# Two-layer decoder trunk on one core: mixer units in another order, query and key products with the weights stationary, rotary on VectorE, and a reordered prologue

## The chip, the cores and the metric

The kernel runs on one core of a Trainium2 chip. The metric is the device time in microseconds: 1187.27 us as the median of 3 runs (1187.05 to 1187.82). TensorE (PE) multiplies into PSUM (8 banks of 128 partitions by 512 fp32 numbers), VectorE (DVE), ScalarE (ACT) and GpSimd (POOL) do the rest, and SyncE (SP) issues the loads of the weights.

## The reference

Two layers, 256 tokens of width 1024, all in fp32. Each layer is

```python
h = h + 0.5 * rms_norm(swiglu(rms_norm(h, g1), w_gu, w_down), g2)          # FFN 1
u = rms_norm(h, mix_pre_g)
sb_q, sb_k, sb_v, df_q, df_k, df_v, g_sb, g_df = split(u @ w_in)           # 6 x 512, 2 x 1024
z = sb_q @ sb_k.T / 8                                                      # 8 heads of 64, strictly causal
w = exp(log_sigmoid(z) + sum of log_sigmoid(-z) over later allowed keys)   # stick-breaking
y_sb = (w @ sb_v) @ w_branch_sb
dq, dk = rope(df_q), rope(df_k)                                            # 4 heads of 2 x 64
a = softmax(dq[0] @ dk[0].T / 8) - lam * softmax(dq[1] @ dk[1].T / 8)      # causal
y_df = (rms_norm(a @ df_v) * (1 - lam_init)) @ w_branch_diff
h = h + rms_norm((sigmoid(g_sb) * y_sb + sigmoid(g_df) * y_df) @ w_out, mix_post_g)
h = h + 0.5 * rms_norm(swiglu(...), ...)                                   # FFN 2
h = h + rms_norm((p @ w_ple_proj) * sigmoid(rms_norm(h, g) @ w_ple_gate), ple_post_g)
```

## The kernel before

**Units.** All weights come in units of 1 MB (128 x 2048), three slots deep. For each unit SP loads `raw`, ACT rounds it to fp32r in `w_hi` (`high`), DVE writes the rest into `w_lo` (`low`), and PE multiplies it. A product is three matmuls: high by high, high by low, low by high. Where the weights move (`exact`, L1473 to L1475, called by `wide` and `deep`), each has 512 columns and the activations of 128 tokens are stationary. In the middle steps of an FFN (`flat_gate_up`) the weights are stationary: a long matmul (L1591) moves high and low parts of all 256 tokens (512 columns), a short one (L1601) the high part (256 columns); the result is transposed (channels by tokens) and its two halves have to be added, and scaled per token by the row `r_cols`. `begin(i, u)` waits until DVE has split unit u; `units_used` gives the slot back.

**Order.** The program of each engine is written out by hand, and each engine runs its instructions in order. The mixer's loop goes over m = 0 to 22. Units 0 to 19 are the ten column blocks of w_in, two half units (rows 0 to 511, 512 to 1023) each; block j is units 2j and 2j+1. In step m PE multiplies unit m for tokens 0 to 127, does `middle(i, m)`, then tokens 128 to 255, then `behind(i, m)`; ACT and DVE in their step m prepare unit m+2, and then do what the tables place there. Stick-breaking slot 2m is in `middle`, 2m+1 in `behind`. So the small attention operations of PE stand between half units of the w_in product.

**Mixer before.** The blocks come as sb_q, sb_k, sb_v, df_q, df_k, df_v and four halves of the gates. ACT copies q and k out of PSUM with the token's scale (`keep`, L842) into `slab`; DVE copies both v (L1314); POOL turns df_q and df_k in `rope` (L577 to L585); PE transposes each of the four with 8 transposes (`turn_four`, L1692), and ACT or DVE copies the result back (L876, L1329). For each pair of stick heads there are scores (`stick_scores`, L1709 and L1712), the sum over later keys (`stick_later`, L1723 and L1724) and values (`stick_values`, L1736), in slots 12, 15, 17 and every 6 slots after; for each differential head a mask matmul in bf16 (`masked`, L1698), scores (L1749, L1752) behind unit 12, 14, 16, 18, transposes of the mixed probabilities (L1759) behind the next unit, and values (L1767 to L1770) in the middle of the one after it. DVE takes the maximum (L1323), mixes (L1344) and scales the outputs (L1278); ACT has the exponentials (L792 to L809), L813 and L823.

**Prologue before.** p and w_ple_proj come in pieces of 128 tokens and of 128 x 512: pieces 0 and 2 and x on ACT's queue, p tile 0, piece 1, p tile 1, piece 3 and then the 12 pieces of the first three FFN units on SP's. PE keeps itself busy with 13 and 5 transposes of the identity (`warm_up`, L1884) about the transpose of p tile 0 (L1877), and does `proj(0)` token tile by token tile with the transposes of x (L1520) and of the gains (L1889 to L1896) between. `high_piece` (L657) and `low_piece` (L1062, L1065) split the pieces; `keep_e` (L670) copies the projection E out of PSUM.

Of the kernel before, what the change touches and what calls it, by code (L numbers as in the profile page):

```python
# [76 lines left out]
def trunk_kernel(nc, a, out):  # L77
    with ExitStack() as ctx:
# [82 lines left out]
        ident_b = sb("ident_b", [P, P], BF16)  # L161
# [3 lines left out]
        mask_df = sb("mask_df", [P, SEQ], BF16)  # L165
# [15 lines left out]
        slab_c = tmp[:, :, W:D]  # L181

# [42 lines left out]
        kept_dve = sem("kept_dve")  # L225
# [3 lines left out]
        sb_turned = sem("sb_turned")  # L229
# [12 lines left out]
        d_score = sem("d_score")  # L242
        d_max = sem("d_max")
# [55 lines left out]
        HT_BANK, P_BANK, FIRST_P_BANK = 6, 7, 3  # L299
# [15 lines left out]
        OUT_COLS = slice(384, W)  # L315
        both_scores = ps[:, 0:2, 0:384]
        both_outs = ps[:, 0:2, OUT_COLS]
# [30 lines left out]
        def p_bank(i):  # L348
            return bank(P_BANK if i else FIRST_P_BANK).rearrange("p (k n) -> p k n", k=2)
# [36 lines left out]
        def _(sp_):  # L386
# [3 lines left out]
            load_p(0)  # L390
# [47 lines left out]
            load_pieces(U_PROJ, (1,))  # L438
            load_p(1)
            load_pieces(U_PROJ, (3,))  # L440
            for u in range(1, PIECED):
                load_pieces(u)
            for i in range(DEPTH):
# [3 lines left out]
                for m in range(20):  # L447
                    dst = raw[:, slot(U_WIN + m), :].rearrange("p (k n) -> p k n", k=4)
                    r0, c0 = (m % 2) * 4 * P, (m // 2) * W
                    src = a["w_in"][bass.ds(i, 1), r0:r0 + 4 * P, c0:c0 + W].rearrange("o (k p) n -> p (o k) n", p=P)  # L450
                    load(i, U_WIN + m, [(dst[:, k:k + 2, :], src[:, k:k + 2, :]) for k in (0, 2)])
# [19 lines left out]
        def _(pool):  # L471
# [19 lines left out]
            pool.memset(ident_b[:, :], 0.0)  # L491
            pool.memset(minus[:, :], -1.0)
            pool.memset(cap_sb[:, :, :], BIG)
            pool.memset(mask_df[:, :], 0.0).then_inc(blank, 1)
            pool.wait_ge(blank, 2)
            pool.affine_select(out=ident_b[:, :], in_=ident_b[:, :], compare_op=ALU.not_equal, fill=1.0,
                               base=0, pattern=[[-1, P]], channel_multiplier=1)

# [6 lines left out]
            for c in (0, P):  # L505

                last = pool.affine_select(out=mask_df[:, c:c + P], in_=mask_df[:, c:c + P],
                                          compare_op=ALU.is_ge, fill=NEG, base=0, pattern=[[-1, P]],
                                          channel_multiplier=1)
            last.then_inc(const_all, 1)  # L510
# [58 lines left out]
            def rope(i, k):  # L569

                for t in range(TT):
                    pool.wait_ge(kept_act, 16 * i + 2 * (2 + k) + t + 1)
                    if k or t:
                        pool.wait_ge(roped, 4 * i + 2 * k + t)
                    x = slab[:, t, :].rearrange("p (g c) -> p g c", c=64)
                    y = rope_b[:, t, :].rearrange("p (g c) -> p g c", c=64)
                    pool.tensor_tensor(slab_c[:, t, :].rearrange("p (g c) -> p g c", c=64), x,  # L577
                                       rope_c[:, t:t + 1, :].to_broadcast([P, 8, 64]), ALU.mult)
                    pool.tensor_tensor(y[:, :, 0:32], x[:, :, 32:64],
                                       rope_s[:, t:t + 1, 0:32].to_broadcast([P, 8, 32]), ALU.mult)  # L580
                    pool.tensor_tensor(y[:, :, 32:64], x[:, :, 0:32],
                                       rope_s[:, t:t + 1, 32:64].to_broadcast([P, 8, 32]), ALU.mult
                                       ).then_inc(rope_parts, 1)
                    pool.wait_ge(rope_parts, 4 * i + 2 * k + t + 1)
                    pool.tensor_tensor(slab[:, t, :], slab_c[:, t, :], rope_b[:, t, :], ALU.add).then_inc(roped, 1)  # L585

            for i in range(DEPTH):
# [11 lines left out]
                pool.wait_ge(rope_ready, 2)  # L599
                rope(i, 0)  # L600
                rope(i, 1)
# [16 lines left out]
        def _(act):  # L618
# [41 lines left out]
            def high_p(i, t=0, toks=slice(0, SEQ)):  # L660

                act.wait_ge(p_turned, nth_p(i, t))
                act.activation(p_hi[:, :, toks], p_bank(i)[:, :, toks], ACT.Copy).then_inc(p_high, 1)
# [56 lines left out]
            def keep_r(i, f):  # L720
                act.wait_ge(r_turned, 2 * i + f + 1)
                act.activation(r_cols[:, 0, :], bank(R_BANK)[:, 0:SEQ], ACT.Copy).then_inc(r_kept, 1)
# [25 lines left out]
            def ffn(i, f, u0, g0, next_unit, loads):  # L748
# [8 lines left out]
                keep_r(i, f)  # L757
# [21 lines left out]
            def stick(i, slot_):  # L779

                if slot_ in SB_VALUE:
                    n = SB_VALUE[slot_]
                    act.wait_ge(s_value, PAIRS * i + n + 1)
                    act.activation(os_hi[:, n, :].rearrange("p (t q) -> p t q", t=TT), both_outs, ACT.Copy
# [13 lines left out]
            def diff_after(i, m):  # L798
                if m >= DF_Z0 and (m - DF_Z0) % 2 == 0 and (m - DF_Z0) // 2 < DF_HEADS:
                    hd = (m - DF_Z0) // 2  # L800
                    act.wait_ge(d_max, DF_HEADS * i + hd + 1)
                    for c in range(2):
# [12 lines left out]
            def diff_mid(i, m):  # L815

                if m >= DF_P0 and (m - DF_P0) % 2 == 0 and (m - DF_P0) // 2 < DF_HEADS:
                    hd = (m - DF_P0) // 2
                    act.wait_ge(d_value, DF_HEADS * i + hd + 1)
                    if hd:  # L820
                        act.wait_ge(d_square, DF_HEADS * i + hd)
# [1137 lines left out]
```

## Time and profile before

| | |
|---|---|
| median of 3 runs | 1187.27 us |
| the profiled execution, its own time | 1187.24 us |
| its span, first to last instruction | 1185.2 us |
| what lies around the span | 2.0 us |
| granted TensorE clock, mean | 0.999 |
| DMA | 215.36 MB, mean 182 GB/s |
| first mixer | about 205 to 345 us of the span and on to the boundary |
| second mixer | about 790 to 930 us and on |

Times are from the span's start. In the chain of waits a piece reads: start, duration, engine, tile, line and how many instructions; pieces follow each other without overlap, so there they show the rate at which PE gets on. In the timeline a matmul's own duration is longer than its share of the chain, since matmuls overlap.

### The profile page before, as it was taken

Reading aid. Unit: us, or ns where it says so; the run is one execution under the profiler, and the core shown is the slowest. Engines: PE = TensorE matmul, PEld = TensorE weight load, DVE = VectorE, ACT = ScalarE, POOL = GpSimd, SP = SyncE. Lnnn points to the kernel's source line nnn. Section 1 sums busy time; section 2 is a strip of 40 time slices with the busy share of each in tenths; the row PEclk is TensorE's granted clock in tenths of the full one; section 3 lists DMA queues with packets and bytes.
Section 4 is the critical chain, followed back from the end, with each engine's and each line's share of the span. In section 5 each row is a group of like instructions: output and inputs, shape, how many; then the busy total and the mean of one; then the engine's idle time right before and its main releaser. Section 6 shows DMA issues by size and latency. Waiting matters only on the chain.

```text
span 1185.2 us, 17137 instructions
## 1 busy us (share of the span) xinstructions
PE 1173.8 (99%) x6013; PEld 984.4 (83%) x6013; DVE 848.7 (72%) x1235; ACT 719.9 (61%) x1163; POOL 92.9 (8%) x157
## 2 busy tenths in 40 slices
PE   8999999999999999999999999999999999999997
PEld 7888888888788888888888888888877888888886
DVE  5766777588667866676787776676976776767666
ACT  6655556666665755564685655576656666555555
POOL 4000000042000100000110000010600010000002
PEclk9999999999999999999999999999999999999999
DMA  8656565553345555556546565756343456556550
GB/s 269 232 183 201 171 218 192 198 178 118 132 178 178 178 196 194 191 172 230 178 158 203 175 209 178 249 162 208 114 159 133 169 178 213 175 179 206 183 196 36
DMA packets 138654, 215.36 MB, mean 182 GB/s; under 512 B 6958, under 2 KB 97904, under 8 KB 138608
## 3 DMA queue, kind: packets, MB, share of 16 engines
q1 hardware_dynamic: 135808, 208.43, 52.9%
q10 hardware_dynamic: 2576, 6.29, 1.6%
q8 instruction: 28, 0.46, 0.2%
q14 instruction: 18, 0.15, 0.0%
q0 software_dynamic: 224, 0.04, 0.0%
HBM read 213.68 MB, written 1.05 MB: 181 GB/s over the span
## 4 chain that ended last, share of the span: by engine, by line
PE 96%; ACT 2%; DVE 1%; DMA 1%; issue 0%; POOL 0%; SPq 0%; DVEq 0%; POOLq 0%; ACTq 0%
PE ps L1591 22%; PE ps L1473 19%; PE ps L1475 19%; PE ps L1474 19%; PE ps L1601 12%; PE ps L1520 2%; PE ps L1692 1%; DMA raw<-in_w_ple_proj 1%; PE ps L1723 1%; DVE w_lo L1084 0%; ACT w_hi L646 0%; PE ps L1736 0%; PE ps L1709 0%; ACT prob L804 0%; PE ps L1752 0%
## 5 line engine op out<-in xcount | busy, mean ns | idle before, releaser
L1084 DVE SCALAR_TENSOR_TENSOR w_lo<-raw,g_layer,w_hi 128x512 fp32r<-128x512 f32 (+1 forms) x504 | 369.6, 793 | 131.4 <-ACT w_hi L646 131.4
L646 ACT ACTIVATE w_hi<-raw,g_layer 128x512 fp32r<-128x512 f32 (+1 forms) x524 | 346.9, 732 | 113.5 <-PE ps L1601 97.0
L1591 PE MATMUL ps<-x_both,w_hi 128*128 128x512 f32 x1152 | 287.7, 392 | 0.0
L1473 PE MATMUL ps<-w_hi,x_both 128*128 128x512 f32 x640 | 257.4, 402 | 0.0
L1475 PE MATMUL ps<-w_hi,x_both 128*128 128x512 f32 x640 | 250.2, 391 | 0.0
L1474 PE MATMUL ps<-w_lo,x_both 128*128 128x512 f32 x640 | 249.6, 390 | 0.0
L1591 PEld LDWEIGHTS ps<-x_both,w_hi 128*128 128x128 f32 x1152 | 209.4, 189 | 39.3 <-issue 0.3
L1081 DVE TENSOR_TENSOR w_lo<-raw,w_hi 128x1024 fp32r<-128x1024 f32 x114 | 134.7, 1221 | 55.0 <-ACT w_hi L643 55.0
L643 ACT ACTIVATE w_hi<-raw 128x1024 fp32r<-128x1024 f32 x114 | 114.7, 1052 | 91.7 <-PE ps L1475 91.6
L1601 PEld LDWEIGHTS ps<-x_both,w_lo 128*128 128x128 f32 x1152 | 152.6, 191 | 8.4
L1601 PE MATMUL ps<-x_both,w_lo 128*128 128x256 f32 x1152 | 156.0, 283 | 0.0
L1473 PEld LDWEIGHTS ps<-w_hi,x_both 128*128 128x128 f32 x640 | 120.2, 188 | 27.1 <-issue 3.3
L1475 PEld LDWEIGHTS ps<-w_hi,x_both 128*128 128x128 f32 x640 | 120.1, 188 | 26.1
L1474 PEld LDWEIGHTS ps<-w_lo,x_both 128*128 128x128 f32 x640 | 120.4, 188 | 22.8
L1473 PE MATMUL ps<-w_hi,ht_hi 128*128 128x512 f32 x320 | 124.9, 390 | 0.0
L1475 PE MATMUL ps<-w_hi,ht_lo 128*128 128x512 f32 x320 | 124.6, 389 | 0.0
L1474 PE MATMUL ps<-w_lo,ht_hi 128*128 128x512 f32 x320 | 124.5, 389 | 0.0
L728 ACT ACTIVATE glu<-glu 128x512 f32<-128x512 f32 x36 | 22.8, 633 | 78.5 <-DVE glu L1130 78.5
L1475 PEld LDWEIGHTS ps<-w_hi,ht_lo 128*128 128x128 f32 x320 | 60.1, 188 | 12.5
L1474 PEld LDWEIGHTS ps<-w_lo,ht_hi 128*128 128x128 f32 x320 | 60.1, 188 | 12.4
L1473 PEld LDWEIGHTS ps<-w_hi,ht_hi 128*128 128x128 f32 x320 | 60.1, 188 | 12.3
L536 POOL TENSOR_TENSOR ms_post<-mean_post,eps_half 128x1 f32<-128x1 f32 x8 | 2.4, 305 | 548.6 <-ACT tmp L694 548.6
(217 smaller groups left out, 1008.7 us busy)
## 6 DMA issues: line engine op xcount, KB each, us to landing
raw<-in_ffn_w_gu SPq DMA_DIRECT2D x170, 512.0 KB, 4.6
raw<-in_ffn_w_down SPq DMA_DIRECT2D x88, 512.0 KB, 4.0
raw<-in_w_in SPq DMA_DIRECT2D x80, 512.0 KB, 4.6
raw<-in_w_out SPq DMA_DIRECT2D x16, 512.0 KB, 3.7
raw<-in_w_ple_gate SPq DMA_DIRECT2D x16, 512.0 KB, 4.1
raw<-in_w_branch_sb SPq DMA_DIRECT2D x8, 512.0 KB, 3.7
raw<-in_w_branch_diff SPq DMA_DIRECT2D x8, 512.0 KB, 3.7
raw<-in_ffn_w_gu SPq DMA_DIRECT2D x12, 256.0 KB, 7.6
```

The costliest lines, as they stand in the source:

```text
L643: last = act.activation(w_hi[:, s, part], raw[:, s, part], ACT.Copy)
L646: last = act.activation(w_hi[:, s, part], raw[:, s, part], ACT.Copy, scale=g_layer[:, g:g + 1])
L728: act.activation(glu_g, glu_g, ACT.Silu).then_inc(silu_done, 2)
L1081: last = dve.tensor_tensor(w_lo[:, s, part], raw[:, s, part], whi[:, part], ALU.subtract)
L1084: last = dve.scalar_tensor_tensor(out=w_lo[:, s, part], in0=raw[:, s, part], scalar=g_layer[:, g:g + 1], in1=whi[:, part], op0=ALU.mult, o ...
L1473: pe.matmul(dst, x_h, w_h, start=first, stop=False, **group)
L1474: pe.matmul(dst, x_h, w_l, start=False, stop=False, **group)
L1475: return pe.matmul(dst, x_l, w_h, start=False, stop=last, **group)
L1520: mm = pe.transpose(x_bank(i, q, idx)[:, k * P:(k + 1) * P], src[:, (4 * n + k) * P:(4 * n + k + 1) * P], ident[:, :])
L1591: mm = pe.matmul(dst, w_hi[:, s, cols], x_both[:, :, 4 * half + k, :], start=half == 0 and k == 0, stop=stop and k == 3, skip_group_check= ...
L1601: mm = pe.matmul(bank(FLAT_BANK[j])[:, 0:SEQ], w_lo[:, s, cols], x_hi[:, 4 * half + k, :], start=False, stop=False, skip_group_check=True)
L1692: mm = pe.transpose(dst[:, k * SEQ + t * P:k * SEQ + (t + 1) * P], src[:, t, k * P:(k + 1) * P], ident[:, :])
```

## The change

The column blocks of w_in come in another order (df_q, df_k, sb_q, sb_k, df_v, sb_v, gates). sb_q and sb_k are multiplied with the weights stationary (`flat_win`); ACT copies one half of each result (`keep_flat`), DVE adds the other and multiplies by the token scales (`add_flat`), which PE transposes once for it at the end of unit 2 (`turn_r`). Their `turn_four` go. Rotary moves to DVE, straight out of PSUM, and its L1314 copies of v go to ACT. The mask matmul goes; DVE caps the diagonal scores in PSUM instead, ahead of the maximum. The tables place stick scores and differential scores together behind units 7, 10, 13, 16, stick later-sums together with the differential transposes in the middle of units 9, 12, 15, 18, and the values of stick pairs in the middle of 12, behind 13 and 16, in the middle of 19, differential values behind 9, 12, 15, 18. Stick outputs have banks of their own. In the prologue the projection is done in the order in which the pieces come, p tile 1 is issued ahead of piece 1, and E is copied earlier. The wait for the first product at the first flat gate-up (banks 6, 7) is left out. At the top of the mixer DVE spreads r_pre for `turn_r`.

```diff
-SBQ, SBK, SBV, DFQ, DFK, DFV = range(6)
+DFQ, DFK, SBQ, SBK, DFV, SBV = range(6)
+W_IN_BLOCK = (3, 4, 0, 1, 5, 2, 6, 7, 8, 9)
 PAIRS = SB_HEADS // 2
-SB_SCORE = {12 + 6 * n: n for n in range(PAIRS)}
-SB_LATER = {15 + 6 * n: n for n in range(PAIRS)}
-SB_VALUE = {17 + 6 * n: n for n in range(PAIRS)}
-DF_Z0, DF_T0, DF_P0 = 12, 13, 14
-BY_ACT = (0, 1, 3, 4, 6, 7, 8, 9)
-QK_ORDER = {SBQ: 0, SBK: 1, DFQ: 2, DFK: 3}
+SB_SCORE = {15 + 6 * n: n for n in range(PAIRS)}
+SB_LATER = {18 + 6 * n: n for n in range(PAIRS)}
+SB_VALUE = {slot_: n for n, slot_ in enumerate((24, 27, 33, 38))}
+DF_SCORE = {7 + 3 * n: n for n in range(DF_HEADS)}
+DF_TURN = {9 + 3 * n: n for n in range(DF_HEADS)}
+BY_ACT = (DFV, SBV, 6, 7, 8, 9)
 PIECED = 4
-WARM_UP = (13, 5)
+WARM_UP = (13, 3)
...
+        SB_FLAT = {SBQ: (0, 4), SBK: (0, 2)}
+        VALUE_BANK = (3, 3, 3, 5)
+        def outs(n):
+            return bank(VALUE_BANK[n])[:, 0:SEQ].rearrange("p (t q) -> p t q", t=TT)
...
-            load_pieces(U_PROJ, (1,))
-            load_p(1)
-            load_pieces(U_PROJ, (3,))
+            load_pieces(U_PROJ, (1, 3))
...
-            def rope(i, k):
...
-                    pool.tensor_tensor(slab[:, t, :], slab_c[:, t, :], rope_b[:, t, :], ALU.add).then_inc(roped, 1)
...
+            def keep_flat(i, j, x):
+                wait_product(act, win_done, 10 * i + j + 1, i, U_WIN + 2 * j + 1, x)
+                act.wait_ge(flat_added, 4 * i + 2 * (j - SBQ) + x)
+                act.activation(flat_copy, flat_pair(SB_FLAT[j][x])[1], ACT.Copy,
+                               scale=SB_D ** -0.5 if j == SBQ else 1.0).then_inc(flat_kept, 1)
...
+                    elif m in (5, 7):
+                        for x in range(2):
+                            high(i, U_WIN + m + 2, 8 + 4 * (m % 2), halves=(x,))
+                            keep_flat(i, m // 2, x)
...
             high_piece(U_PROJ, 0)
             high_p(0, 0, slice(0, P))
+            high_piece(U_PROJ, 2)
+            high_p(0, 1, slice(P, SEQ))
             high_piece(U_PROJ, 1)
-            high_p(0, 1, slice(P, SEQ))
-            high_piece(U_PROJ, 2)
             high_piece(U_PROJ, 3)
             load_x(1)
             high_inputs(0, 0, 0, (0,))
             high_inputs(0, 0, 1, (0,))
             high_piece(1, 3)
             high_piece(2, 0)
+            for t in range(TT):
+                keep_e(0, t)
+            high_piece(2, 1)
             high_inputs(0, 0, 0, (1,))
-            high_piece(2, 1)
             high_piece(2, 2)
-            keep_e(0, 0)
+            high_piece(2, 3)
+            high_piece(3, 0)
+            high_piece(3, 1)
             high_inputs(0, 0, 1, (1,))
-            high_piece(2, 3)
             square_pre(0, 0, 0)
-            keep_e(0, 1)
-            for k in range(4):
-                high_piece(3, k)
+            high_piece(3, 2)
+            high_piece(3, 3)
             first_silu(0, 0, U_FFN1)
...
+            def rope(i, k, t):
+                wait_product(dve, win_done, 10 * i + k + 1, i, U_WIN + 2 * k + 1, t)
+                r = (r_query, r_pre)[k][:, t:t + 1]
+                x = bank(WIN_BANK[k][t]).rearrange("p (g c) -> p g c", c=64)
+                y = rope_b[:, t, :].rearrange("p (g c) -> p g c", c=64)
+                dve.scalar_tensor_tensor(out=slab_c[:, t, :].rearrange("p (g c) -> p g c", c=64), in0=x, scalar=r,
+                                         in1=rope_c[:, t:t + 1, :].to_broadcast([P, 8, 64]),
+                                         op0=ALU.mult, op1=ALU.mult)
+                for lo, hi in ((0, 32), (32, 64)):
+                    last = dve.scalar_tensor_tensor(out=y[:, :, lo:hi], in0=x[:, :, 32 - lo:64 - lo], scalar=r,
+                                                    in1=rope_s[:, t:t + 1, lo:hi].to_broadcast([P, 8, 32]),
+                                                    op0=ALU.mult, op1=ALU.mult)
+                last.then_inc(rope_parts, 1)
+                dve.wait_ge(rope_parts, 4 * i + 2 * k + t + 1)
+                dve.tensor_tensor(df_slabs[k][t], slab_c[:, t, :], rope_b[:, t, :], ALU.add).then_inc(roped, 1)
+            def add_flat(i, j, x):
+                n = 4 * i + 2 * (j - SBQ) + x + 1
+                dst = (sbq_t, sbk_t)[j - SBQ][:, 2 * x:2 * x + 2, :]
+                dve.wait_ge(flat_kept, n)
+                dve.scalar_tensor_tensor(out=dst, in0=flat_pair(SB_FLAT[j][x])[0],
+                                         scalar=SB_D ** -0.5 if j == SBQ else 1.0, in1=flat_copy,
+                                         op0=ALU.mult, op1=ALU.add).then_inc(flat_added, 1)
+                dve.wait_ge(flat_added, n)
+                dve.wait_ge(r_kept, nth_r(i, 1))
+                dve.tensor_tensor(dst, dst, r_cols.to_broadcast([P, 2, SEQ]), ALU.mult).then_inc(sb_ready, 1)
...
+                    if m - 1 in DF_TURN:
+                        diff_normed(i, DF_TURN[m - 1])
+                    stick_cap(i, 2 * m)
+                    if m in (1, 3):
+                        rope(i, m // 2, 1)
...
+                        for c in range(2):
+                            last = dve.tensor_tensor(diagonal(DF_BANK[c]), diagonal(DF_BANK[c]),
+                                                     cap_df[:, :, :].to_broadcast([P, 2, P]), ALU.min)
+                        last.then_inc(d_capped, 1)
+                        dve.wait_ge(d_capped, DF_HEADS * i + hd + 1)
...
-            def masked(b, mask):
-                pe.matmul(diagonal(b), ident_b[:, :], mask[:, :].rearrange("p (a n) -> p a n", a=2), start=True,
-                          stop=False, skip_group_check=True)
...
-                pe.wait_ge(sb_turned, 2 * i + 2)
+                pe.wait_ge(sb_ready, 4 * i + 3 + n // 2)
                 if n:
-                    pe.wait_ge(os_split, PAIRS * i + n)
+                    pe.wait_ge(s_weight, PAIRS * i + n)
...
+                kept(i, (SBV, SBV, 7, 8)[n], 1)
+                if n:
+                    pe.wait_ge(os_split, PAIRS * i + n)
...
+            def flat_win(i, m, j, half, x):
+                s, b = slot(U_WIN + m), SB_FLAT[j][x]
+                if half == 0:
+                    if x:
+                        pe.wait_ge(rope_parts, 4 * i + 2 * (j - SBQ) + 2)
+                    elif j == SBK:
+                        pe.wait_ge(flat_added, 4 * i + 1)
+                def long(stop):
+                    for n in range(2):
+                        dst = bank(b + n).rearrange("p (a n) -> p a n", a=2)
+                        for k in range(4):
+                            cols = slice(k * W + (2 * x + n) * P, k * W + (2 * x + n + 1) * P)
+                            mm = pe.matmul(dst, w_hi[:, s, cols], x_both[:, :, 4 * half + k, :],
+                                           start=half == 0 and k == 0, stop=stop and k == 3, skip_group_check=True)
+                    return mm
+                def short():
...
+            def bank_free(i, j, t):
+                if j in (DFV, SBV):
+                    pe.wait_ge(flat_added, 4 * i + 2 * (j - DFV) + 2)
+                elif j > SBV:
+                    kept(i, j - 2, t)
+                    if t == 1 and j in (7, 9):
+                        pe.wait_ge(os_split, PAIRS * i + {7: 2, 9: 3}[j])
...
+            def first_proj():
+                beside = {(0, 1): lambda: (turn(0, 0, 0), turn_first_gain()), (0, 3): lambda: turn(0, 0, 2),
+                          (1, 3): turn_gains}
+                for t, k in ((0, 0), (0, 2), (1, 0), (1, 2), (0, 1), (0, 3), (1, 1), (1, 3)):
+                    if (t, k) in beside:
+                        beside[t, k]()
+                    if k == 0:
+                        pe.wait_ge(p_split, nth_p(0, t))
+                    if t == 0 and k < 3:
+                        pe.wait_ge(piece_split, (0, 2, 1).index(k) + 1)
+                    if (t, k) == (0, 3):
+                        begin(0, U_PROJ)
+                    cols, toks = piece(U_PROJ, k), slice(t * P, (t + 1) * P)
+                    mm = exact(bank(E_PAIR[t] + k // 2), p_hi[:, k % 2, toks], p_lo[:, k % 2, toks],
+                               w_hi[:, slot(U_PROJ), cols], w_lo[:, slot(U_PROJ), cols], k % 2 == 0, k % 2 == 1)
+                    if (t, k) == (0, 3):
+                        mm.then_inc(e_done, 1)
+                mm.then_inc(units_used, 1)
```

ACT's `keep` now serves df_v, sb_v and the gates; ACT copies both turned df tiles (behind units 4 and 6). DVE's prologue list follows ACT's.

## Rows read from the trace of the kernel before

**Rows 1.** The page, busy time by engine: us, share of span, instructions.

```profile
PE 1173.8 (99%) x6013; PEld 984.4 (83%) x6013; DVE 848.7 (72%) x1235; ACT 719.9 (61%) x1163; POOL 92.9 (8%) x157
```

**Rows 2.** The page, the chain that ended last, by engine.

```profile
PE 96%; ACT 2%; DVE 1%; DMA 1%; issue 0%; POOL 0%; SPq 0%; DVEq 0%; POOLq 0%; ACTq 0%
```

**Rows 3.** Waits of PE: line, releaser, us in total, times, longest.

```profile
PE ps L1767 <- ACT mixed_t L813: 0.4, 2, 0.2
```

**Rows 4.** The chain of waits in the first mixer: start, us, what.

```profile
218.82 0.87 PE ps L1692 x8
...
239.68 0.63 PE ps L1709 x4
240.31 0.22 PE ps L1712 x4
240.53 0.43 PE ps L1473
...
256.37 0.43 PE ps L1473
...
284.55 0.23 PE ps L1698 x2
284.78 0.42 PE ps L1749 x4
...
295.95 0.24 PE ps L1770 x2
...
298.00 0.61 DVE glu L1278 x2
...
315.83 0.36 PE ps L1698 x2
```

**Rows 5.** The chain of waits over one step of the FFN loop.

```profile
45.33 1.81 PE ps L1591 x8
...
56.48 0.23 PE ps L1473
...
61.92 1.81 PE ps L1591 x8
```

**Rows 6.** Busy time, mixer: columns us; PE, PEld, DVE, ACT, POOL busy; clock, DMA, GB/s.

```profile
205.00:345.00 140.00, 139.79 (x729) 112.69 (x728) 101.83 (x156) 94.18 (x181) 26.29 (x29) 1.00 0.48 162
```

**Rows 7.** Groups of DVE in the first mixer: busy us, mean ns, idle before.

```profile
L1241 DVE SCALAR_TENSOR_TENSOR soft<-ps,soft 128x768 f32<-128x768 f32 x4 | 3.8, 956 | 4.1 <-ACT soft L796 4.1
```

**Rows 8.** Timeline of DVE in the first mixer: start, us, line, operation.

```profile
222.01 2.74 DVE L1084 SCALAR_TENSOR_TENSOR w_lo<-raw,g_layer,w_hi 128x512 fp32r<-128x512 f32 x4 [2.74 <-ACT w_hi L646]
...
246.44 4.78 DVE L1084 SCALAR_TENSOR_TENSOR w_lo<-raw,g_layer,w_hi 128x512 fp32r<-128x512 f32 x4
```

**Rows 9.** Groups of POOL in the first mixer.

```profile
L577 POOL TENSOR_TENSOR tmp<-tmp,rope_c 128x512 f32<-128x512 f32 x4 | 5.6, 1403 | 43.3 <-ACT tmp L842 43.0
```

**Rows 10.** Groups of ACT in the first mixer.

```profile
L845 ACT ACTIVATE gates<-ps,r_pre 128x512 f32<-128x512 f32 x8 | 5.0, 673 | 0.0
```

**Rows 11.** The chain of waits, prologue.

```profile
27.93 1.81 PE ps L1591 x8
...
30.70 2.00 PE ps L1591 x8
```

**Rows 12.** Issue to landing, two p tiles (issued 0.8, 1.7).

```profile
DMA to landing us min/median/max: 2.9/4.2/5.5
```

**Rows 13.** Issue to landing, w_ple_proj pieces 0 and 2 (issued 0.8, 1.3).

```profile
DMA to landing us min/median/max: 3.1/4.1/5.1
```

**Rows 14.** Issue to landing, first six w_gu pieces (issued 2.7 to 6.6).

```profile
DMA to landing us min/median/max: 7.6/7.6/7.9
```

**Rows 15.** Timeline of the prologue.

```profile
4.84 0.99 PE L1884 MATMUL ps<-ident 128*128 128x128 f32 x5
...
6.32 0.39 PE L1474 MATMUL ps<-w_lo,p_hi 128*128 128x512 f32 x1
...
13.35 1.32 ACT L657 ACTIVATE w_hi<-raw,g_layer 128x512 fp32r<-128x512 f32 x2
```

More of the change, by code:

```diff
@@ L181, in trunk_kernel @@
         slab_c = tmp[:, :, W:D]
+        df_slabs = [[x[:, t, 0:W] for t in range(TT)] for x in (tmp, gates[:, 0, :, :])]
+        flat_copy = w_att[:, :, 0:SEQ]
         minus = mixed_t[:, 0:P]
@@ new lines, in diff_keep, with diff_square @@
+            def diff_keep(i, hd):
+                act.wait_ge(d_turned, DF_HEADS * i + hd + 1)
+                act.activation(mixed_t[:, :], bank(DF_BANK[0])[:, 0:384], ACT.Copy).then_inc(d_kept, 1)
+            def diff_square(i, hd):
+                act.wait_ge(d_value, DF_HEADS * i + hd + 1)
+                if hd:
+                    act.wait_ge(d_square, DF_HEADS * i + hd)
+                for t in range(TT):
+                    last = act.activation(squares[:, t * P:(t + 1) * P], bank(DF_BANK[1])[:, t * P:(t + 1) * P],
+                                          ACT.Square, scale=DF_V ** -0.5, accum_out=mean_sub[:, t:t + 1])
+                last.then_inc(d_square, 1)
@@ L1285, in mixer @@
                     elif 2 * m in SB_VALUE:
-                        low(i, U_WIN + m + 2, 8 + 4 * (m % 2), halves=(0,))
+                        gain = 8 + 4 * (m % 2) if m < 18 else None
+                        low(i, U_WIN + m + 2, gain, halves=(0,))
                         stick_out(i, 2 * m)
-                        low(i, U_WIN + m + 2, 8 + 4 * (m % 2), halves=(1,))
+                        low(i, U_WIN + m + 2, gain, halves=(1,))
+                    elif m in (5, 7):
+                        for x in range(2):
+                            low(i, U_WIN + m + 2, 8 + 4 * (m % 2), halves=(x,))
+                            add_flat(i, m // 2, x)
                     elif m < 18:
@@ L1575, in ffn, with flat_gate_up @@
             def ffn(i, f, q, u0, before_last):
-                def flat_gate_up(u, half, step, c=0):
+                def flat_gate_up(u, half, step, c=0, first=False):
                     begin(i, u, c)
@@ L1580, in flat_gate_up @@
                     for js in ((0, 1), (2, 3)):
-                        if half == 0:
+                        if half == 0 and not (first and js == (0, 1)):
                             pe.wait_ge(prod_done, 4 * NC * i + 2 * NC * f + 2 * step + js[0] // 2 - 1)
@@ L1745, in diff_scores @@
                     pe.wait_ge(d_normed, DF_HEADS * i + hd)
-                for c in range(2):
-                    masked(DF_BANK[c], mask_df)
                 for c, rows in enumerate(HEAD_ROWS):
-                    pe.matmul(bank(DF_BANK[c])[:, 0:P], dfq_t[rows, hd, 0:P], dfk_t[rows, hd, 0:P], start=False,
+                    pe.matmul(bank(DF_BANK[c])[:, 0:P], dfq_t[rows, hd, 0:P], dfk_t[rows, hd, 0:P], start=True,
                               stop=False, skip_group_check=True)
@@ new lines, in flat_win @@
+            def flat_win(i, m, j, half, x):
[14 more added lines that the diff above has]
+                def short():
+                    for n in range(2):
+                        for k in range(4):
+                            cols = slice(k * W + (2 * x + n) * P, k * W + (2 * x + n + 1) * P)
+                            mm = pe.matmul(bank(b + n)[:, 0:SEQ], w_lo[:, s, cols], x_hi[:, 4 * half + k, :],
+                                           start=False, stop=False, skip_group_check=True)
+                    return mm
+                if half == 0:
+                    long(False)
+                    return short()
+                short()
+                mm = long(True)
+                if x == 0:
+                    mm.then_inc(win_done, 1)
+                return mm
```

293 lines of the change are left out of this document (123 added, 170 removed).

## The prediction

> **What bounds the kernel now.** I read the busy times first: PE is busy for 1173.8 of 1185.2 us [rows 1]. Busy time alone would not settle it, since matmuls overlap, so next the chain that ended last: 96% of it is PE [rows 2]. Then PE's waits: in both mixers together it waits 0.4 us, at two places, for ACT's copy of the turned probabilities [rows 3]. The other waits lie in the first 11 us and the tail. So only three things can move the time: the work in PE's own queue, the prologue until PE runs without a gap, and new waits that the new order makes. DVE and ACT are busy for 102 and 94 of 140 us of a mixer [rows 6]: what they gain or lose counts only where PE comes to stand.
>
> **The mixer, PE's work per layer.** Prices are steps of the chain.
>
> 1. Turns of q and k. Eight transposes take 0.87 us [rows 4]; four such groups become two: -1.74.
> 2. Masks. Four pairs of bf16 matmuls at 0.23 or 0.36 us [rows 4]; I take 0.27, nearer to the more frequent value: -1.08 (-0.9 to -1.4).
> 3. Scores beside scores. Four stick score matmuls with 128 columns take 0.22 us, four differential ones of the same shape 0.42, right behind the mask [rows 4]: 0.20 for entering the 64-row form. The first full matmul behind the stick scores takes 0.43 us [rows 4] where one takes 0.23: 0.20 for leaving it. With the two kinds of scores in a row behind units 7, 10, 13, 16, one entry and one exit go per head: 4 x 0.40 = -1.60 (0 if the cost is per group, not per change).
> 4. Values ahead of scores, behind units 13 and 16. Behind values the full matmul also takes 0.43 [rows 4]. One of the two exits goes at each place: 2 x 0.20 = -0.40 (0 to -0.8). The Trainium skill (TensorEngine Tiling, Tiling Modes, Key Properties) says that changing the tiling mode drains the array, not only changing the tile. Values and scores differ in their form, so by that rule a change stays between them and the term is 0.40; if they counted as one form it would be 0.80.
> 5. `turn_r`: two transposes, a quarter of 0.87: +0.22.
> 6. Flat blocks. A loop step takes 61.92 - 45.33 = 16.59 us, of which the down product, 24 matmuls, takes 61.92 - 56.48 = 5.44, so 0.227 each. The flat pair of units is 16.59 - 5.44 = 11.15 us [rows 5]; as a wide pair it would be 48 x 0.227 = 10.88. Two blocks: +0.54. The columns are equal in number, but the flat form has 64 instructions for 48.
> 7. A new wait. Differential values of head 0 now stand right behind unit 9, and their third group needs tile 1 of df_v, which ACT can only begin to copy when unit 9 ends. That copy takes 0.67 us [rows 10], the matmuls ahead of it about 2 x 0.22: +0.30 (0 to 0.7, if ACT is behind by one more copy). Behind it are PE's whole queue and unit 10.
>
> Sum: -1.74 - 1.08 - 1.60 - 0.40 + 0.22 + 0.54 + 0.30 = -3.76, for two layers -7.5. PE's wait for the turned probabilities goes, since the values come half a unit after the turn: -0.4 [rows 3]. The wait left out at the first flat gate-up I cost at nothing: that first group takes 1.81 us in the prologue as in the loop [rows 5, 11], so nothing waited there.
>
> **The mixer, the other engines.** Rotary is 4 instructions per token tile (512, 256, 256, 512 columns). DVE's nearest row is 956 ns for 768 columns out of PSUM [rows 7], which makes some 0.7, 0.35, 0.35, 0.7: 2.1 us, four times, 8.4 in all. Its upper bound is POOL's own 1.40 for 512 columns [rows 9], so 5.2 per tile. `add_flat` is 2 x 0.7, four times: 5.6. The caps are 8 at 0.35 to 0.45, about 3.2. The v copies and the copies of the turned df tiles leave DVE (about 5.3). Against this, four pieces of `w_lo` take 2.74 us alone and 4.78 while POOL runs rotary [rows 8], and POOL is busy for 26.3 us of this stretch [rows 6]; the Trainium skill (SBUF — State Buffer, Who interferes with whom) calls this an exclusive lock on a shared port pair, for DVE instructions with two SBUF inputs, and by it all of the excess goes. I take it as 10 us back. DVE's net is then +2 and at the upper prices +14 of 140: there is room. Cover in detail: DVE splits two units ahead of PE, 10.9 us. In steps 1 and 3 it has 2.74 + 2 x 2.1 = 6.9 us, in 2 and 4 2.74, a mean of 4.8 against PE's 5.45. Without this cover the cost is item for item: at POOL's prices steps 1 to 4 hold 32 us against 22, and nearly all of the lead is gone.
>
> The tightest new place is the first stick score, behind unit 7. SBK's first half is done in the middle of unit 7; ACT copies (0.6), DVE adds and scales (1.4), while the low half of unit 9 (1.4, behind ACT's copy of a turned tile) may stand ahead. I count 5.2 us from the start of unit 7, PE asks at 5.6: no wait, margin 0.4. The next is DVE's scaling of head n, needed by the scores of head n+1. Before, it came 298.61 - 296.19 = 2.4 us after the values with DVE idle ahead of it [rows 4]. Now ACT starts `high` of the next unit only behind the squares (0.65) and DVE scales behind its `low`: about 0.65 + 2.6 + 0.8 + 0.6 = 4.7 us after the values, and PE asks a unit later, at 5.45. Margin 0.75, at units 10, 13, 16. The copies of q and k that leave ACT (8) and those that come (4 flat, 4 v) balance.
>
> **The prologue.** p tile 1 was issued at 1.7 and landed 5.5 later, at 7.2 [rows 12]; issued 0.46 earlier and ahead of 256 KB, it lands before 6.7. Piece 2 lands at 1.3 + 5.1 = 6.4 [rows 13]; ACT splits a piece in 0.66, DVE in 0.7 [rows 8, 15], so PE has it at 7.75. From there nothing is late: seven groups of three projection matmuls and 48 of the gate-up, 69 x 0.23 = 15.9, four turns of x at 0.44 (half of 0.87), the gains 0.3: 7.75 + 15.9 + 1.75 + 0.3 = 25.7 for the first flat group, which began at 27.93 [rows 11]. The weights allow it: the w_gu pieces land from 2.7 + 7.9 = 10.6 to 6.6 + 7.6 = 14.2 [rows 14], and with ACT at 0.66 and DVE at 0.7 per piece, the copy of the gains between, piece 3 is split at about 16.0, where PE wants it at 16.1. E's copies (2 x 1 us) now stand ahead of piece 5 on ACT, where it waited for x before. Gain 2.2. The second flat group waited 0.16 for the product of token tile 1 (2.00 against 1.84) [rows 11]; ACT's chain to that product moves forward by less than PE does, to about 28.95, and the group would start at 28.5: 0.4, so +0.25. Sum -1.95 (-0.3 if a landing holds it, -2.4).
>
> **The forecast.** -7.5 - 0.4 - 1.95 = -9.9. The profiled execution took 1187.24 us, 0.03 below the median: 1177.3 us. Its own range is 1175 to 1179.5, from the bounds of items 2, 4, 7 and the prologue.
>
> **Rivals.**
>
> A. The changes of form cost nothing when joined, since the 0.20 is a start-up of each group. Then items 3 and 4 vanish: +4.0, 1181.3. For: the 0.42 stands behind a bf16 matmul, another kind of operand. Against: the exit is seen on a full matmul, which is no group of its own.
>
> B. PE's clock comes late in the prologue. The five transposes of the warm-up take 0.99 us, 0.20 each, and eight in the mixer 0.87, 0.11 each [rows 4, 15]: the first ran at the lower level (1.2 GHz), and by 6.32 a matmul takes the 0.39 us that all take [rows 15]. So the level rose just behind the warm-up. With two transposes fewer and then a gap until p tile 1 has landed, it may stay low for the first four projection groups: 12 x 0.23 more, less the 0.5 of idle time this fills, +2.3: 1179.6. The Trainium skill (TensorE: Matmul & The Clock Gate, Part 4: PE-mode transpose) says that transposes don't count as work for the gate. By that rule the warm-up never did anything and the level would always be low at the first projections; the row at 6.32 says otherwise, with only transposes before.
>
> C. The prologue is held by landings: 1178.9 to 1179.2.
>
> D. Slower. The scaling of a differential head stands behind `low`, that behind `high`, that behind the squares, and these behind PE's values, a closed loop three times per layer. It decides from 0.75 us of lateness on. If DVE's steps in which the cap (0.8), the maximum (1.0), the stick softplus (3.3) and the mixing (1.2) meet run 3 us late, each of six places costs 2.25: +13.5, 1190.8. For: these now fall in one step. Against: a head's loop has three units for it, 16.4 us and the small operations, where it had two.
>
> E. Small waits at several of these places, 3 to 6 us in all: 1180 to 1183.5.
>
> **Chances.** Forecast 0.65, A 0.08, B and C 0.10, E 0.10, D 0.07. Less than 0.2% (2.4 us) can't be told from no change here. Faster by more: forecast, A, B, C and nearly all of E, 0.89. Within: 0.04. Slower: 0.07. Range 1174.5 to 1182.5: it takes in A, B, C and half of E.
>
> **What would show it.** The first flat group at 25.7 us. In the mixer: no 0.42 for the differential 128-column scores behind stick scores; a wait of PE for ACT's copy of v_df of about 0.3; four pieces of w_lo in 2.74 throughout; no waits of PE for L1278's successor or for the token-scaled q and k. The mixer from its start to the start of FFN 2 about 4 us shorter. The forecast is wrong if PE waits for DVE in the mixer for more than 1 us per layer, or if the first matmuls of the projection are 0.46 apart.

## The result, and the profile after

The changed kernel takes 1175.96 us (median of 5 runs, 1175.88 to 1176.14) where the kernel before takes 1187.44 us on the same chip (5 runs, 1187.05 to 1187.82): ratio 0.9903 [0.9892, 0.9914], 11.5 us less. The forecast was 1177.3 us, that is 9.9 less, with a range of 1174.5 to 1182.5. The profiled execution took 1175.95 us, its span 1174.2 us. From the page, busy times and the chain that ended last by engine, the answer to [rows 1, 2]:

```profile
PE 1164.3 (99%) x6031; PEld 983.6 (84%) x6031; DVE 849.9 (72%) x1289; ACT 720.6 (61%) x1165; POOL 52.1 (4%) x122
PE 99%; ACT 0%; DVE 0%; POOL 0%; issue 0%; DVEq 0%; POOLq 0%; ACTq 0%
```

PE has 9.5 us less to do and is on 99% of the chain instead of 96%. What it waits for (us in total, times, longest), answering to [rows 3]:

```profile
PE ps L1958 <- POOL ident L489: 1.6, 1, 1.6
PE ps L1801 <- ACT v_df L827: 0.7, 2, 0.3
PE ps L1506 <- DVE p_lo L1404: 0.4, 1, 0.4
```

In the mixers the only wait is the one that item 7 announced, 0.3 per layer; the old one on the turned probabilities is gone. The first mixer in the chain of waits (start, duration, what), answering to [rows 4]. L1867 and L1876 are the long and the short matmuls of the flat blocks, L1727 is `turn_four`, L1739 and L1742 the stick scores, L1779 and L1782 the differential ones, L1768 the stick values, L1801 the third group of differential values, L1506 the first of three wide matmuls:

```profile
221.88 1.81 PE ps L1867 x8
...
239.47 0.87 PE ps L1727 x8
...
245.93 0.63 PE ps L1739 x4
...
246.79 0.22 PE ps L1779 x4
247.01 0.43 PE ps L1782 x4
247.44 0.43 PE ps L1506
...
260.06 0.70 ACT v_df L827
260.80 0.49 PE ps L1801 x2
...
288.01 0.81 PE ps L1768 x12
288.82 0.63 PE ps L1739 x4
```

The differential 128-column scores stand at 246.79 and take 0.22 behind stick scores, where they took 0.42 behind the mask. The only long step behind the two groups is one exit, 0.43 at 247.44. To place the gain in time I took the last flat group of each FFN; in front of the second FFN lies a whole mixer. Before:

```profile
170.79 1.84 PE ps L1591 x8
...
540.15 1.84 PE ps L1591 x8
```

and after:

```profile
168.13 1.84 PE ps L1626 x8
...
533.31 1.84 PE ps L1626 x8
```

2.66 us are gained before the first mixer, 6.84 behind it: the prologue gives 2.66 and the first mixer 4.18. About the second mixer the same groups stand at 755.27 and 1124.62 before, at 748.52 and 1113.69 after: 6.75 and 10.93, again 4.18. The spans differ by 11.0, so 0.1 lies in the tail. Around the span lie 1.75 us where it was 2.0 (0.3), and the last 0.2 up to the 11.5 of the medians is spread of the runs.

### The profile page after: what moved, and what is told of

Read it like the earlier page. It is cut to its first block, busy times and chain, and to the rows that moved or that the text cites. A ratio compares the mean times of both kernels' runs of the same rounds, so it can differ in the third digit from the quotient of the medians.

```text
span 1174.2 us, 17191 instructions
## 1 busy us (share of the span) xinstructions
PE 1164.3 (99%) x6031; PEld 983.6 (84%) x6031; DVE 849.9 (72%) x1289; ACT 720.6 (61%) x1165; POOL 52.1 (4%) x122
## 4 chain that ended last, share of the span: by engine, by line
PE 99%; ACT 0%; DVE 0%; POOL 0%; issue 0%; DVEq 0%; POOLq 0%; ACTq 0%
PE ps L1626 23%; PE ps L1506 19%; PE ps L1508 18%; PE ps L1507 18%; PE ps L1636 12%; PE ps L1867 2%; PE ps L1553 2%; PE ps L1876 1%; PE ps L1753 1%; PE ps L1768 1%; PE ps L1727 0%; PE ps L1739 0%; PE ps L1782 0%; PE ps L1958 0%; PE ps L1789 0%; PE ps L1801 0%
## 5 line engine op out<-in xcount | busy, mean ns | idle before, releaser
L1077 DVE SCALAR_TENSOR_TENSOR w_lo<-raw,g_layer,w_hi 128x512 fp32r<-128x512 f32 (+1 forms) x504 | 356.4, 767 | 139.0 <-ACT w_hi L632 139.0
L1506 PE MATMUL ps<-w_hi,x_both 128*128 128x512 f32 x576 | 231.1, 401 | 0.0
L1508 PE MATMUL ps<-w_hi,x_both 128*128 128x512 f32 x576 | 225.1, 391 | 0.0
L1507 PE MATMUL ps<-w_lo,x_both 128*128 128x512 f32 x576 | 224.6, 390 | 0.0
L1506 PEld LDWEIGHTS ps<-w_hi,x_both 128*128 128x128 f32 x576 | 108.2, 188 | 24.1 <-issue 3.0
L1508 PEld LDWEIGHTS ps<-w_hi,x_both 128*128 128x128 f32 x576 | 108.1, 188 | 23.5
L1507 PEld LDWEIGHTS ps<-w_lo,x_both 128*128 128x128 f32 x576 | 108.4, 188 | 20.6
L1506 PE MATMUL ps<-w_hi,ht_hi 128*128 128x512 f32 x320 | 125.0, 390 | 0.0
L1506 PEld LDWEIGHTS ps<-w_hi,ht_hi 128*128 128x128 f32 x320 | 60.1, 188 | 12.3
L1125 DVE TENSOR_TENSOR glu<-glu,prob 128x512 f32<-128x512 f32 x36 | 24.9, 692 | 27.6 <-ACT glu L714 27.6
```

The costliest lines, as they stand in the source:

```text
L1077: last = dve.scalar_tensor_tensor(out=w_lo[:, s, part], in0=raw[:, s, part], scalar=g_layer[:, g:g + 1], in1=whi[:, part], op0=ALU.mult, o ...
L1125: dve.tensor_tensor(glu_g, glu_g, wide_r, ALU.mult).then_inc(silu_scaled, 1)
L1506: pe.matmul(dst, x_h, w_h, start=first, stop=False, **group)
L1507: pe.matmul(dst, x_h, w_l, start=False, stop=False, **group)
L1508: return pe.matmul(dst, x_l, w_h, start=False, stop=last, **group)
```

## The experiments

Six of the eight kernels change one thing in the changed kernel or bring one part of it to the kernel before; e5 is a repeat and e8 joins two repairs. e1 to e4 ran beside each other, and so did e5 to e8. The changed kernel took 1175.96 for the result and 1176.37 as e5, so 0.4 us is what one kernel differs by from itself between groups, and a difference is given against both where it is small.

**e1: the prologue alone**, in the kernel before: `WARM_UP = (13, 3)`, p tile 1 ahead of piece 1, `first_proj`, E's copies early.

```diff
-            load_p(0)
+            for t in range(TT):
+                load_p(t)
...
+            for t in range(TT):
+                keep_e(0, t)
...
-            keep_e(0, 0)
...
-            keep_e(0, 1)
```

> The kernel before with the new prologue alone (load order, projection in order of arrival, E copied early, warm-up 13 and 3); the mixer as before. Theory: the gain of the prologue is its own and is kept to the end, since PE never waits afterwards. In the changed kernel the last flat group of FFN 1 ends 2.66 us earlier, so this kernel takes 2.6 us less than before, about 1184.8. Rival: the prologue only moves a wait (weights of the first mixer or the first layer's end are not there earlier), then it is within 0.5 us of before.

1184.96 us (1184.3 to 1185.46, 10 runs), ratio 0.9977 [0.9968, 0.9986] to 1187.38: 2.4 less. The first flat group began at 25.87 where it began at 27.93 [rows 11]. What the prologue gains is kept to the end. The rest is 9.0 us: 8.4 in the two mixers (2 x 4.18), and 0.6 by which the first flat group began earlier still in the changed kernel's own profile (25.31).

**e2: the two kinds of scores apart.** Three of the four stick score groups go to the middle of a unit.

```diff
-SB_SCORE = {15 + 6 * n: n for n in range(PAIRS)}
+SB_SCORE = {15: 0, 20: 1, 26: 2, 32: 3}
```

> The changed kernel with the stick scores of pairs 1, 2 and 3 half a unit earlier, in the middle of units 10, 13, 16, and the differential scores left behind these units; pair 0 stays joined. Theory (0.20 us for each change into or out of the 64-row form): 6 heads x 0.40 = +2.4 us against the changed kernel, 1178.4. Rival (joining costs and gives nothing, the 0.20 was a start-up of each group): 0, 1176.0. If an early stick score must wait for the weights of the pair before, more than +2.4.

1178.67 us (1178.49 to 1179.12, 5 runs), ratio 0.9925 [0.9911, 0.9938]: 2.7 more than the changed kernel, 2.3 more than its repeat. The chain of waits:

```profile
264.81 0.43 PE ps L1506
...
267.78 0.42 PE ps L1779 x4
...
268.64 0.43 PE ps L1506
```

The same eight differential matmuls now cost an entry of 0.20 (0.42 for 0.22) and leave behind them a second exit of 0.20 (0.43 for 0.23): 0.40, six times 2.4. That is the price of a change of form, not of a group: rival A is out.

**e3: a bf16 matmul between them.** The mask matmuls are put back behind the stick scores; DVE's cap stays, so in the mixer only PE's side changes.

```diff
+                for c in range(2):
+                    pe.matmul(diagonal(DF_BANK[c]), ident_b[:, :], mask_df[:, :].rearrange("p (a n) -> p a n", a=2),
+                              start=True, stop=False, skip_group_check=True)
```

> The changed kernel with the two bf16 mask matmuls put back ahead of each pair of differential scores, so between stick scores and differential scores; DVE's cap stays too. Theory (the 0.20 is for a change of form): 0.27 for the masks, 0.40 for one more exit and entry, 8 heads: +5.4 us, 1181.4. Rival (start-up per group): the masks alone, 8 x 0.27 = +2.2, 1178.2.

1180.53 us (1180.26 to 1180.73, 5 runs), ratio 0.9939 [0.9925, 0.9953]: 4.6 more (4.2 against the repeat).

```profile
247.01 0.33 PE ps L1789 x2
247.34 0.42 PE ps L1792 x4
247.76 0.43 PE ps L1795 x4
248.19 0.43 PE ps L1516
```

A mask in the middle costs 0.33 of its own and 0.20 for entering the scores again (L1792: 0.42), 0.53 per head and 4.2 for eight heads. I had expected 5.4, with a whole exit of 0.20 on the small matmuls; they took 0.33 behind scores where most took 0.23 behind wide ones [rows 4], 0.10 more. The change of form therefore costs both ways again, but less into a small bf16 group than into a wide matmul. The Trainium skill (TensorEngine Tiling (Array Packing), Tiling Modes, Key Properties) says that a change of mode drains the array and a change of tile doesn't; e2 and e3 agree that the changes cost time, at 0.20 us for each side of fp32 work and 0.10 into the bf16 pair.

**e4: ACT's copy of v in two parts**, head 0's 128 columns first, so that PE's third value group waits for a quarter of the copy.

```diff
+                        if (j, t) == (DFV, 1):
+                            act.activation(dst[:, 0:DF_V], bank(WIN_BANK[0][1])[:, 0:DF_V], ACT.Copy,
+                                           scale=r_pre[:, 1:2]).then_inc(kept_head, 1)
...
-                kept(i, DFV, 1)
+                if hd == 0:
+                    pe.wait_ge(kept_head, i + 1)
+                else:
+                    kept(i, DFV, 1)
```

> The changed kernel with ACT's copy of token tile 1 of df_v in two parts, the 128 columns of head 0 first, and PE's values of head 0 waiting for that part alone. Theory: in the chain of the changed kernel the new wait costs 0.70 + 0.04 + 0.49 - 0.66 = 0.57 us per layer; the first part takes about 0.3, less than the 0.44 of PE's matmuls ahead, so both waits go: -1.1 us, 1174.8. Rival: the wait only moves to the restart of PE or to ACT, whose squares come later by the second part: 0 to -0.4.

1175.65 us (1175.53 to 1175.75, 4 runs), ratio 0.9898 [0.9883, 0.9913]: 0.3 less, 0.7 less than the repeat, where 1.1 less was expected. The chain, and PE's load of the weights for the third group from the timeline:

```profile
260.62 0.22 PE ps L1805 x2
260.85 0.01 issue
260.86 0.49 PE ps L1811 x2
```

```profile
260.86 0.30 PEld L1811 LDWEIGHTS ps<-v_df,mixed_t 128*128 128x128 f32 x2 [0.20 <-ACT v_df L827]
```

The wait has shrunk to 0.01, but the third group still takes 0.49 where the two before it take 0.22 each. From the end of the unit to the next wide matmul it was 1.25 us (260.04 to 261.29) and is 0.95. So a wait has two prices in the chain: its own length, and 0.27 for starting again. The second stayed here because the first part of the copy was done only when PE had finished the group ahead: the load of the weights still stood 0.20 us for ACT. No run has the copy done early enough to show both prices gone. The kernel before has the same start on another line, its wait for the turned probabilities: there the first group of head 1 took 0.49, that of head 2, which waited for nothing, 0.22:

```profile
311.01 0.49 PE ps L1767 x2
...
326.78 0.22 PE ps L1767 x2
```

The prediction priced both waits, the old one and the new, by their length alone.

**e5: the changed kernel again**, as the measure for e6 to e8.

> The changed kernel itself, as the yardstick of this group: 1176.0 us. The start of the first flat group differs from profile to profile with the landing of the first pieces (25.2 to 25.9 us so far), so 0.3 us of spread is expected and no more.

1176.37 us (1176.21 to 1176.43, 4 runs), ratio 0.9908 [0.9893, 0.9924] to 1187.14. Its profile lists a small wait of the prologue that the first did not list. In its chain, DVE's work for the pieces of the first FFN unit (the gains are copied from 13.09 to 13.47):

```profile
14.21 0.60 DVE x_both L1102
14.81 0.67 DVE w_lo L1058
...
15.52 0.50 PE ps L1506
```

The copies of the gains and x's second tile stand ahead of the piece that PE needs next, and PE asks at 15.3. In the changed kernel's first profile the same matmul takes 0.49 (at 15.22) without a listed wait: PE came just to a stand there too. The wait is 0 to 0.2 us from one execution to the next.

**e6: POOL busy in the mixer.** Twenty products of 128 x 256 in SBUF per layer, from unit 5 on; nobody reads them.

```diff
+                for n in range(20):
+                    if i or n:
+                        pool.wait_ge(pool_step, 20 * i + n)
+                    pool.tensor_tensor(pool_out[:, :], pool_in[:, :], pool_in[:, :], ALU.mult).then_inc(pool_step, 1)
```

> The changed kernel with 20 two-input operations of 128x256 on POOL per layer, from the end of SBQ's first half (unit 5) on, on tiles that nobody reads: POOL is as busy there as it was with rotary. Theory: VectorE's time was never the limit, so the pieces of w_lo take up to 4.8 us per four again and the kernel loses nothing but at the tightest place, the first stick score (0.5 us of margin in the changed kernel): 0 to +2 us, 1176 to 1178. Rival (clearing POOL was a part of the 11.5 us): +4 us or more.

1177.38 us (1177.27 to 1177.57, 5 runs), ratio 0.9917 [0.9904, 0.9931]: 1.0 more than e5. PE's waits, the stick scores in the chain, and DVE's timeline (start, duration, line, operation) about the flat sums:

```profile
PE ps L1748 <- DVE sbk_t L1308: 1.0, 2, 0.5
```

```profile
246.67 0.70 PE ps L1748 x4
```

```profile
238.01 4.16 DVE L1086 SCALAR_TENSOR_TENSOR w_lo<-raw,g_layer,w_hi 128x512 fp32r<-128x512 f32 x4
...
245.54 1.07 DVE L1308 TENSOR_TENSOR sbk_t<-sbk_t,prob 128x512 f32<-128x512 f32 x1
```

Four pieces take 4.16 in place of 2.74, and `add_flat`'s multiplication 1.07 in place of 0.69. The first stick score (L1748) waits 0.5 per layer. That is where I had put the tightest margin, 0.4 us, and it is what breaks first. Behind the wait the scores take 0.70 where they take 0.63 without one: 0.07 more, and not 0.27, so starting again and entering the scores (0.20) are not paid one on top of the other. The Trainium skill (SBUF — State Buffer, Who interferes with whom) says that a DVE instruction with two SBUF inputs contends with a GpSimd instruction that reads SBUF; the run agrees. The size: this load on POOL costs 1.0 of the 11.5 us. It is lighter on DVE than rotary was (4.16 for 4.78 [rows 8]), and no run puts rotary itself back on POOL in this order; but at this size a quiet POOL is a small part of the gain, not its source.

**e7: no warm-up.** PE has only the four transposes of p ahead of the projection.

```diff
-WARM_UP = (13, 3)
+WARM_UP = (0, 0)
```

> The changed kernel without any transpose of the identity ahead of and between the transposes of p. Theory (the transposes raised the clock, which in the changed kernel is at its upper level by 5.9 us): the first projections run at 0.46 us per matmul for some 3 to 4 us, so about 8 matmuls x 0.23 late, +1.5 to +2.5 us, a little less if the landings hide it. Rival (transposes do not count for the clock): the first projections of the changed kernel would not have been fast, or 0 us of change here.

1177.89 us (1177.69 to 1178.28, 5 runs), ratio 0.9921 [0.9908, 0.9935]: 1.5 more than e5.

```profile
5.80 0.73 PE ps L1506
...
10.37 0.43 PE ps L1507
10.80 0.24 PE ps L1508
...
27.22 1.81 PE ps L1626 x8
```

The first eleven matmuls go at the lower level (1.2 GHz): one of 0.73 behind a wait, ten of 0.43. From 10.80 it is 0.23 to 0.24, the upper level. The column of the granted clock shows 1.00 for this stretch too (us from:to, length, busy of PE, PEld, DVE, ACT, POOL, clock, DMA share, GB/s), so the level has to be read from the steps:

```profile
5.80:10.80 5.00, 5.00 (x13) 3.87 (x13) 2.41 (x4) 1.77 (x4) 1.80 (x10) 1.00 1.05 337
```

In the changed kernel, with 16 identity transposes ahead, nearly all steps from 5.88 on are 0.23. The Trainium skill (TensorE: Matmul & The Clock Gate, Part 4: PE-mode transpose) says that the gate's full rate doesn't engage for transposes, which don't count as busy in the same way. For this kernel's fp32 transposes of the identity the run disagrees: with only transposes taken away, the first eleven matmuls ran at half speed. Rival B named 2.3 us for twelve slow matmuls less the idle time; eleven cost 1.5. In the changed kernel's profile two transposes fewer did not bring it about; e8 shows a small piece of it.

**e8: both repaired.** e4's copy in two parts, and DVE splits the last two pieces of the first FFN unit ahead of the gains and of x's second tile.

```diff
-            keep_gains()
             low_piece(1, 2)
-            low_inputs(0, 0, 1, (0,))
             low_piece(1, 3)
+            keep_gains()
+            low_inputs(0, 0, 1, (0,))
```

> The changed kernel with the df_v copy in two parts (as in e4) and, in the prologue, DVE's copies of the remaining gains and the low half of x's second tile behind the fourth piece of the first FFN unit, not ahead of it. In all profiles of the changed prologue PE waits at 15.2 to 15.7 us for that fourth piece, 0.4 us. Theory: -0.3 per layer from the first, -0.4 from the second: -1.0 us against e5, 1175.0. Rival: the second tile of x is then late for PE, or a landing is what counts in the prologue: -0.5.

1175.53 us (1175.11 to 1175.63, 4 runs), ratio 0.9900 [0.9885, 0.9915]: 0.8 less than e5 where 1.0 was expected, the fastest of all, though by only 0.1 against e4. e4's part alone gave 0.7 less than e5, so what DVE's new order adds is not shown. PE waits for nothing but the identity at the start, but in this execution the first three projection matmuls ran slow:

```profile
6.11 0.66 PE ps L1513
6.77 0.43 PE ps L1514
...
25.66 1.81 PE ps L1633 x8
```

The steps of 0.23 begin at 7.58. Its first flat group begins at 25.66 and not at 25.31 as in the changed kernel's first profile. There a transpose took 0.21 up to 4.6 us and 0.11 from 4.8 on, so with the same transposes ahead the level rose nearly 3 us earlier; what sets the moment stays open. Over the seven profiles of the changed kernel and its variants with these transposes (all but e7) the first flat group begins at 25.22 (e2) to 25.69 (e4): 0.5 us differs from one execution to the next, by the level (e8) and by the fourth group of pieces (e5).

## Why the prediction was right

The direction and the size came from PE's own queue, and that was the right place: PE stood still for 0.4 us in both mixers before and for 0.7 after. I summed PE's steps by line, each from the end of one instruction to the end of the next, which is what the chain prints, between the last flat group of FFN 1 and the first of FFN 2: 224.59 us before, 220.40 after. So a change of form falls to the first group behind it. Per layer:

| step of the prediction | forecast | measured |
|---|---|---|
| 1 and 5, turns and `turn_r` | -1.52 | -1.53 |
| 2, masks | -1.08 | -1.15 |
| 3, entries into the differential scores | -0.80 | -0.80 |
| 3 and 4, exits: seen on the wide matmuls | -1.20 | -1.46 |
| the old wait, on the differential values | -0.20 | -0.48 |
| 6, flat instead of wide | +0.54 | +0.54 |
| 7, the new wait, on the differential values | +0.30 | +0.60 |
| sum | -3.96 | -4.28 |

Another +0.09 lie in other lines, so the difference is -4.19 per layer: the mixers gave 8.4 where 7.9 was forecast. The rows of items 1, 5 and 6 rest on this count alone; no run takes them back one by one.

**Items 1 and 2** are right: the groups went, with the price that the rows gave.

**Item 3** is shown by e2 and e3, entry by entry. **Item 4** was the lower of its two values: behind unit 13 the stick scores take 0.63 behind values (288.82) as they do behind a flat block (245.93), so the entry stayed and only the exit of the values went. In the middle of unit 12 values are followed by later-sums, and there the exit fell to these: L1753 takes 0.38 at 277.47 where it takes 0.17 behind a wide matmul at 255.84. These 0.21 are in the other lines; against them stands one such exit into transposes that is gone.

**Exits.** The wide matmuls lost 1.46 us beyond the 96 that went (839 to 743 of them, 193.86 to 170.65 us, and 96 x 0.2267 = 21.76). The steps of 0.43 among them went from 11 to 5, six exits as forecast, 1.20. Of the other 0.26, 0.11 are two steps of 0.28 behind later-sums that are gone too; the rest is spread over the remaining steps.

**Item 6** was right to the hundredth: from 221.88 to 245.93 in the chain, less two `turn_four` of 0.87, the flat blocks take 22.31, 0.55 more than 21.76.

**Item 7 and the old wait** were both undersized, since the prediction priced a wait by its length alone. The new wait is 0.3 as said, and starting again behind it 0.27; the old one was 0.2, and 0.27 behind it. Both prices were too low by about 0.3, and they cancel because one wait went and one came. That is luck: had the new order only added a wait, each layer would have been 0.3 off.

**DVE's cover** held. Rotary, per tile of tokens, and `add_flat`:

```profile
208.84 0.74 DVE L1278 SCALAR_TENSOR_TENSOR tmp<-ps,r_query,rope_c 128x512 f32<-128x512 f32 x1
...
211.00 2.73 DVE L1077 SCALAR_TENSOR_TENSOR w_lo<-raw,g_layer,w_hi 128x512 fp32r<-128x512 f32 x4
...
244.71 0.69 DVE L1299 TENSOR_TENSOR sbk_t<-sbk_t,prob 128x512 f32<-128x512 f32 x1
```

From 208.84 to 211.00 it is 2.2 us for a forecast of 2.1, and four pieces take 2.73 right behind it, as they did when POOL was silent [rows 8]. The flat sum is ready at 245.40 and PE asks at 245.93: a margin of 0.5 for 0.4 forecast. Rival D's loop kept its distance too:

```profile
265.87 0.60 DVE L1267 TENSOR_SCALAR glu<-ps,r_sub 128x128 f32<-128x128 f32 x2
```

It ends at 266.47, and the scores that need it begin at 267.62, 1.15 us later for a forecast of 0.75. The windows view says the same of the mixer as a whole, answering to [rows 6]:

```profile
202.30:338.10 135.80, 135.47 (x739) 112.51 (x738) 102.90 (x183) 95.15 (x182) 5.76 (x13) 1.00 0.50 171
```

DVE is at 102.9 us with rotary, the flat sums and the caps on it, and POOL at 5.8 where it had 26.3.

**The prologue** gained 2.62 to the first flat group (25.31; forecast 25.7) where 2.2 was forecast, and the 0.25 that I had charged for the second group did not fall due. From the chain:

```profile
5.88 0.50 PE ps L1506
...
6.84 0.32 PE ps L1506
...
9.58 0.43 PE ps L1506
...
15.22 0.49 PE ps L1506
...
25.31 1.81 PE ps L1626 x8
...
28.08 1.96 PE ps L1626 x8
```

The second long group took 1.96, so it waited 0.12; before, 0.16 [rows 11]. The time of the first flat group was nearly right for reasons that I had wrong, and by luck: I held PE back to 7.75 by the landing of piece 2, and it runs from 5.88 with no more than small stops. The two p tiles landed 2.8 to 3.5 us after their issue, where the rows had up to 5.5 [rows 12], and ACT began to split piece 2 at 5.26:

```profile
DMA to landing us min/median/max: 2.8/3.2/3.5
```

In what order the queues served them no run here separates. The start 1.87 us earlier brought only 0.4. The first group of three matmuls (0.69), which the forecast had ahead of its 7.75, now lies behind the start; and the four steps above take 0.82 more than 0.23 each: starting again at 5.88 and 15.22 (0.27 and 0.26), a short stop at 6.84 (0.09), and 0.20 at 9.58 behind the turn of the first gain. The forecast had none of these four at a price.

Together: the forecast of 9.9 fell 1.6 short of the 11.5. The prologue gave 2.66 for 1.95, the mixers 8.4 for 7.9, and the other 0.4 to 0.5 are the tail, the time around the span and the spread of the runs, which no item of the forecast covers. Of rivals C and E nothing showed: the first flat group came early, and PE has no further waits in the mixers.

## What to carry to other kernels

When the chain is 99% one engine, count that engine's instructions and its changes of form; the price of a change can be read before it is made, as the difference between the first and the later steps of the same shape. Put groups of one form side by side and let another engine take the mask. And look at what stands ahead of the tightest hand-over on the engine that makes it: the margin that I had named as the smallest (0.4 us) was the one that gave way when DVE was slowed (e6).

## What the runs showed of the hardware

Transposes of the identity bring PE to its upper level: without them eleven matmuls ran at the lower one, ten of them 0.43 apart and not 0.23, at 1.5 us in all (e7), while the granted clock showed 1.00. The moment of the rise differed by nearly 3 us between two executions with the same transposes ahead (e8). Leaving the 64-row form costs 0.20 us into a wide matmul and 0.10 into two small bf16 ones (e3). Where PE comes to stand, the first step behind it takes 0.27 more: 0.49 for 0.22 behind waits of 0.3 (changed kernel), 0.2 (before) and 0.01 (e4, where the load of the weights had stood 0.20); 0.50 for 0.23 on a wide matmul (e5, at 15.52). Where that step pays for entering the scores anyway, only 0.07 came on top (0.70 for 0.63, e6).
